# Beginning the attention of a second model's mixer earlier, with compression, gates and the first up products between its units

## The reference

```python
# xn: 256 x 1024, normed; projections of it by w_in: NSA queries (8 heads), keys and values of NSA,
# MoBA queries, keys, values (8 heads), 24 gate columns, two wide gates (2 x 1024 columns)
kc, vc = silu(blocks(k) @ ck_w1) @ ck_w2, silu(blocks(v) @ cv_w1) @ cv_w2     # compression
o_c = softmax(q @ kc.T) @ vc                                                  # compressed branch
y_nsa  = g0 * o_c + g1 * attend(q, k_sel, v_sel) + g2 * attend(q, k_win, v_win)   # g = sigmoid(24 columns)
y_moba = attend(q_m, k_m, v_m)
merged = sigmoid(gate_a) * (y_nsa @ w_up_nsa) + sigmoid(gate_b) * (y_moba @ w_up_moba)
x = x + merged @ w_out
```

## Time and profile before

| | |
|---|---|
| median of 3 runs (lowest, highest) | 1749.6 us (1748.1, 1751.0) |
| profiled execution | 1749.17 us, of which the span in the profile is 1747.4 us |
| PE busy | 1684.5 us, 96% |
| DVE busy | 1141.9 us, 65% |
| ACT busy | 892.0 us, 51% |
| mean granted PE clock | 0.991 |
| second mixer | kc's first product at 1273.05 us of the span, next norm's first product at 1518.31 us |

### The profile page before, as it was taken

How to read it: one execution, slowest core, us unless ns; L and a number is a source line. 1 busy time by engine, 2 the same in 40 slices (tenths; PEclk the granted TensorE clock), 3 DMA queues, 4 the chain that set the end, 5 groups by cost and what they waited for, 6 DMA issues and landing times.

```text
span 1747.4 us, 30010 instructions
## 1 busy us (share of the span) xinstructions
PE 1684.5 (96%) x12938; PEld 1544.5 (88%) x12938; DVE 1141.9 (65%) x1622; ACT 892.0 (51%) x1172; POOL 330.2 (19%) x387
## 2 busy tenths in 40 slices
PE   8999999999999997999999999999989899999998
PEld 7978999888999986899998878999978788899998
DVE  5556689756776679566666556767675657754555
ACT  6545555545456664455555545555544446444344
POOL 1211799501560016100000113010006000000000
PEclk9999999999999999999999999999999999999999
DMA  7436547465544653445555334655535521465551
GB/s 249 145 110 178 178 164 243 168 204 169 168 146 169 210 183 109 154 151 187 193 180 174 129 121 111 229 190 173 193 127 165 170 86 62 146 214 184 181 190 49
DMA packets 203396, 286.21 MB, mean 164 GB/s; under 512 B 6432, under 2 KB 162272, under 8 KB 203264
## 3 DMA queue, kind: packets, MB, share of 16 engines
q1 hardware_dynamic: 197584, 272.25, 47.1%
q0 software_dynamic: 2224, 5.75, 1.4%
q10 hardware_dynamic: 3456, 6.29, 1.1%
HBM read 279.03 MB, written 5.24 MB: 163 GB/s over the span
## 4 chain that ended last, share of the span: by engine, by line
PE 85%; DVE 9%; ACT 3%; issue 2%; POOL 1%; DMA 0%; ACTq 0%; SPq 0%; POOLq 0%; DVEq 0%
PE ps L106 84%; DVE wlo L118 3%; ACT arena L112 2%; DVE arena L118 1%; ACT whi L112 1%; PE ps L109 1%; DVE arena L136 1%; DVE xres L118 1%; POOL arena L118 1%; DVE arena L130 1%; POOL sm L118 1%; DVE arena L124 1%; DVE arena L121 0%; DVE sm L121 0%; DVE arena L127 0%
## 5 line engine op out<-in xcount | busy, mean ns | idle before, releaser
L118 DVE TENSOR_TENSOR wlo<-raw,whi 128x2048 fp32r<-128x2048 f32 (+2 forms) x259 | 603.1, 2336 | 294.9 <-ACT whi L112 294.7
L106 PE MATMUL ps<-xh,whi 128*128 128x256 f32 x2288 | 652.8, 285 | 5.3 <-DVE wlo L118 2.4
L106 PE MATMUL ps<-xl,whi 128*128 128x256 f32 x2288 | 648.6, 283 | 0.0
L106 PE MATMUL ps<-xh,wlo 128*128 128x256 f32 x2288 | 648.6, 283 | 0.0
L112 ACT ACTIVATE whi<-raw 128x2048 fp32r<-128x2048 f32 (+2 forms) x259 | 491.6, 1901 | 243.8 <-PE ps L106 241.0
L106 PEld LDWEIGHTS ps<-xh,whi 128*128 128x128 f32 x2288 | 440.0, 192 | 14.7 <-issue 8.9
L106 PEld LDWEIGHTS ps<-xl,whi 128*128 128x128 f32 x2288 | 440.2, 192 | 1.6
L106 PEld LDWEIGHTS ps<-xh,wlo 128*128 128x128 f32 x2288 | 440.1, 192 | 0.0
L106 PE MATMUL ps<-whi,oh 128*128 128x512 f32 (+1 forms) x640 | 249.0, 389 | 2.5 <-DVE wlo L118 1.8
L106 PE MATMUL ps<-wlo,oh 128*128 128x512 f32 (+1 forms) x640 | 247.0, 386 | 0.0
L106 PE MATMUL ps<-whi,ol 128*128 128x512 f32 (+1 forms) x640 | 246.4, 385 | 0.0
(11 more groups left out here) (150 smaller groups left out, 1704.9 us busy)
## 6 DMA issues: line engine op xcount, KB each, us to landing
raw<-in_ffn_w_up SPq DMA_DIRECT2D x88, 1024.0 KB, 5.1
raw<-in_ffn_w_down SPq DMA_DIRECT2D x44, 1024.0 KB, 5.0
raw<-in_sb_w_qkv SPq DMA_DIRECT2D x23, 1024.0 KB, 5.7
raw<-in_w_ffn_in SPq DMA_DIRECT2D x22, 1024.0 KB, 5.1
raw<-in_w_in SPq DMA_DIRECT2D x19, 1024.0 KB, 5.3
raw<-in_w_ffn_out SPq DMA_DIRECT2D x11, 1024.0 KB, 4.9
raw<-in_sb_w_o SPq DMA_DIRECT2D x8, 1024.0 KB, 5.0
raw<-in_sg_w_in SPq DMA_DIRECT2D x8, 1024.0 KB, 5.3
```

Of the source, the lines that this page charges most:

```text
L106: return NOP if self.e is None else self.e.matmul(*a, **k)
L118: return NOP if self.e is None else self.e.tensor_tensor(*a, **k)
```

## The change

**The first tile after a norm by k.** In `qk`, the state-space layer, the up products of every feed-forward net and `kc`, the first tile's 48 matmuls are no longer ordered m outside, k inside, but k outside and m inside (`feat_major_pair`), with the wait for piece k of the normed input (`xl`) ahead of each k. In `tok_major` (of these, the gating layer alone uses it with a wait) the wait for the last piece becomes one for each k:

```diff
     def tok_major(self, pe, w, nk, k0, nK, ah, al, outs, n, xl_of=None):
 
-        if xl_of is not None:
-            pe.wait_ge(*self.on("xl", xl_of, k0 + nk - 1))
         for k in range(nk):
+            if xl_of is not None:
+                pe.wait_ge(*self.on("xl", xl_of, max(k0 + k, 1)))
```

**The attention loop begins after turns 3 to 6**, and everything else goes into it:

```diff
-        block("mix", 24)
...
-        for p in range(3):
-            to_QT(p, ("rope_nsa",))
+        self.heads_turn_pe(pe, V, 5, ("qt_dve", 3))
+        self.heads_turn_pe(pe, V, 6, ("qt_act", 4))
         self.attend_pe(pe, N, V)
...
+    TURN = {4: 0, 5: 1, 6: 2}
+    C_TURN, C_HIDDEN, C_MEAN, C_ROPE, C_TABLES, C_SCORES, C_PROB, C_PC, C_VALUES, Y_SIDE = 7, 8, 9, 10, 11, 12, 13, 14, (18, 19), {15: 2, 16: 3}
...
+            if n < 24 and n % 2 == 0:
+                fronts(n)
+            if n < 4:
+                compress(*self.CMP[n])
+            elif n < 20:
+                gate(*divmod(n - 4, 2))
+            if n == 20:
+                w0 = self.tile(pe, "mup", 0)
+                pe.wait_ge(*self.on("gz_out", 7))
+                self.merge_pe(pe, w0, 0, 0)
+            if n == 21:
+                pe.wait_ge(*self.on("cmp_out", 1))
+                self.merge_pe(pe, w0, 0, 1)
+            if n == 24:
+                w2 = self.tile(pe, "mup", 2)
+                pe.wait_ge(*self.on("a_max", 22))
+                self.merge_pe(pe, w2, 2, 0)
```

```diff
+            if n < 4:
+                self.cut_hi(ac, ("cmp",) + self.CMP[n])
+            elif n < 20:
...
+            if n == 4:
+                ac.wait_ge(*self.on("tile", "cmp", 1, 1))
+                ac.activation(V["HT"], self.B[6][0:30, :], ACT_F.Silu).then_inc(*self.up("ht"))
...
+            if n < 4:
+                self.cut_lo(dv, ("cmp",) + self.CMP[n])
+            elif n < 20 and n % 2 == 0:
+                self.cut_lo(dv, ("gz", (n - 4) // 2))
...
+            if n == 2:
+                dv.wait_ge(*self.on("turn_rstd", 0))
+                self.scale_heads(dv, V, 0, 12).then_inc(*self.up("nsa_scaled"))
+            if n == 3:
+                dv.wait_ge(*self.on("nsa_scaled"))
+                self.rope_heads(dv, N, V, 0, 12, "rope_dve", ("rope_nsa",), "RSN")
```

More of the change, by code:

```diff
@@ L2041, in second_pe @@
-        pe.wait_ge(*self.on("vv_n", 1))
-        for p in range(3):
-            to_QT(p, ("rope_nsa",))
+        self.heads_turn_pe(pe, V, 3, ("rope_moba",))
+        self.heads_turn_pe(pe, V, 4, ("rope_moba",))
+        w = self.tile(pe, "mix")
+        pe.wait_ge(*self.on("head_out", "qn", 1))
+        for k in range(KT):
+            ins = self.mm3(pe, B[2][0:24, 0:256], w[0][:, k, :], w[1][:, k, :], self.xh[:, k, :], self.xl[:, k, :], k == 0, k == KT - 1)
+        ins.then_inc(*self.up("tile", "mix"))
@@ L2061, in second_pe @@
-        for i in range(1, 4):
-            self.out_proj_pe(pe, "second", i)
-    def y_turn_pe(self, pe, V, p, bank):
-        src = V["OA"].rearrange("p t h d -> p t (h d)")
-        if p == 0:
-            pe.wait_ge(*self.on("a_norm", 23))
-            pe.wait_ge(*self.on("gz_out", 7))
-        if p == 1:
-            pe.wait_ge(*self.on("ol", "y", 3))
-        if p == 2:
-            pe.wait_ge(*self.on("a_norm", 3))
-            pe.wait_ge(*self.on("cmp_out", 1))
-        if p == 3:
-            pe.wait_ge(*self.on("a_norm", 7))
-            pe.wait_ge(*self.on("ol", "y", 2))
+                self.merge_pe(pe, w, i, s)
@@ L2077, in y_turn_pe, with heads_turn_pe @@
+        for i in range(4):
+            self.out_proj_pe(pe, "second", i, [("gate_mul", 1, 1)])
+    def heads_turn_pe(self, pe, V, p, done):
+        pe.wait_ge(*self.on(*done))
         for k in range(2):
             for t in range(2):
-                kt = 2 * p + k
-                ins = pe.transpose(self.B[bank][:, k * 256 + t * P:k * 256 + (t + 1) * P], src[:, t, kt * P:(kt + 1) * P], self.ident[:, :])
+                j = 2 * p + k
+                ins = pe.transpose(self.B[self.QT_OUT[p][1]][:, k * 256 + t * P:k * 256 + (t + 1) * P],
+                                   V["QK"][:, t, 2 * j:2 * j + 2, :].rearrange("p a b -> p (a b)"), self.ident[:, :])
+        ins.then_inc(*self.up("qt_turned", p))
@@ new lines, in gate, with mix_turn @@
+        def gate(i, m):
+            if m == 0:
+                self.w_gate = self.tile(pe, "gz", i)
+                pe.wait_ge(*(self.on("gz_out", i - 1) if i else self.on("ht")))
+            ins = self.feat_major(pe, self.w_gate, m, 8, B[6][:, m * 256:(m + 1) * 256], self.xh, self.xl)
+            if m == 1:
+                ins.then_inc(*self.up("tile", "gz", i))
+        def mix_turn():
+            pe.wait_ge(*self.on("mix_sig"))
+            for t in range(2):
+                ins = pe.transpose(B[3][:, 24 * t:24 * t + 24], V["GTF"][:, t * P:(t + 1) * P], self.ident[0:24, 0:24])
+            ins.then_inc(*self.up("mix_turned"))
@@ L2283, in second_act @@
-        for i in range(1, 4):
+        ac.activation(V["GTF"], B[2][0:24, 0:256], ACT_F.Sigmoid).then_inc(*self.up("mix_sig"))
+        self.heads_turn_act(ac, V, 6)
+        self.attend_act(ac, N, V)
+        for i in (1, 3):
+            self.cut_hi(ac, ("mup", i))
+            for s in range(2):
+                s2 = i - 1 + s
+                ac.wait_ge(*self.on("gate_sum", s2))
+                ac.activation(self.xh[:, 2 * s2:2 * s2 + 2, :], V["GZ"][0][s2], ACT_F.Copy).then_inc(*self.up("oh", "second", s2))
@@ L2464, in second_dve @@
-        for i in range(1, 4):
+                s2 = i - 1 + s
+                gz = V["GZ"][0][s2]
+                self.gate_dve(dv, V, i, s)
+                dv.wait_ge(*self.on("gate_mul", i, s))
+                dv.tensor_tensor(gz, gz, V["GZ"][1][s2], ALU.add).then_inc(*self.up("gate_sum", s2))
+                dv.wait_ge(*self.on("oh", "second", s2))
+                dv.tensor_tensor(self.xl[:, 2 * s2:2 * s2 + 2, :], gz, self.xh[:, 2 * s2:2 * s2 + 2, :].bitcast(F32),
+                                 ALU.subtract).then_inc(*self.up("ol", "second", s2))
```

395 lines of the change are left out of this document (204 added, 191 removed).

## The result

The changed kernel takes 1775.9 us (median of 4 runs, 1772.5 to 1777.6) where the kernel before takes 1750.3 us (1748.1 to 1751.0): ratio 1.0145, 95% interval 1.0132 to 1.0158, 25.6 us slower. The forecast was slower by 13.7 us, 1763, with a range up to 1771.

The account below looks back on a forecast made before the run. The prediction took PE to bound the kernel before. Entry +13.5, gated units +3.2, tail -2.2 and first tiles by k -0.8 gave +13.7 us on 1749.17, so 1763 us; own range 1756 to 1769, with rivals 1750 to 1771.

Parts of the forecast that it names:

- The entry: End of `kvn` to first gate: DVE's serial iterations with cuts delay the first gate from 1366.79 to 1380.3, +13.5 us.
- The clock: Half clock behind the stall at the entry: 1.7 to 3.4 us more, 1.7 taken.
- The gated units: First gate to last: eight pairs at 9.5 us plus compressed-branch steps and turns, 85.4, with clock 87, against 83.9: +3.2 us.
- The 6.8 us of the paired fronts are lost here: Gated units: PE work saved by issuing two units' scores together is lost to the chain through DVE and ACT.
- The tail: Behind the gated units to the next norm: 65.4 us, 10.4 of it waits, against 67.6: -2.2 us.
- First tiles by k: Gating layer's 0.79 us wait for pieces of `xl` goes: -0.8 us, nothing taken elsewhere.
- Gate columns: 48 products at 0.11 us become 24 at 0.12, 2.9 us: -2.5 us of PE; first half-clock stretch goes, -3.4.
- the rule on turns: Tail, iterations 24 to 27: turns not counting as busy for the clock would add some 2 us; left out.
- PE bound behind the first gate: Rival, chance 0.10: a pair's chain is hidden, gated units cost 80 us, tail waits halve; +1.5, 1751 us.
- Faster: Rival, chance 0.06: first four units hidden, entry under 15 us, all PE savings count; -21 us, 1728.
- Worse: Rival, chance 0.14: half clock follows each longer wait and a pair's chain is 10.5 us; +7 to +12 more, 1770 to 1775.

Follow-up runs that it names:

- second: Changed kernel with ACT's weight cut moved ahead of the exponentials of its unit, n = 0 to 24: 1749.7 us, ratio 0.9997.
- ninth: Changed kernel with ACT's cut ahead of the exponentials in iterations 0 to 4 only: 1760.7 us, ratio 1.0068.
- third experiment: Changed kernel with 44 and 88 useless products filling PE's two long waits at the entry: 1771.4 us, ratio 1.0126.
- sixth: Changed kernel with ACT's cuts first, plus DVE's last cut and gate products and ACT's four sigmoids deferred behind the loop: 1743.3 us, ratio 0.9962.
- fifth experiment: Kernel before with only the first tiles ordered by k and the gating layer's wait for each k: 1749.8 us, ratio 0.9999.
- seventh: Changed kernel with ACT's cuts first, plus compression's silu taken in iteration 3 instead of 4: 1742.9 us, ratio 0.9967.
- fourth: Kernel before with only the scores of two units issued together at even n: 1748.0 us, ratio 0.9990.
- eleventh: Kernel before with paired scores and ACT's cut ahead of the exponentials: 1741.1 us, ratio 0.9952.
- first experiment: Changed kernel with the scores of each unit issued alone again: 1778.1 us, ratio 1.0160.
- eighth kernel: Changed kernel with ACT's cuts first, deferred tail, earlier silu, and second compressed-branch values an iteration later: 1732.9 us, ratio 0.9905.

## Why the prediction was wrong, and where it was right

**The entry** (+13.5): right in mechanism and size, +13.2. The maximum of unit 4 begins 36.0 us behind the end of `kvn` (forecast 36.4), DVE's cuts follow each other at 6.0, 5.9, 8.2 and 7.7 us where I had 6.1, 5.9, 8.25 and 7.85 for the iterations, the waits of 5.5 and 11.0 us for the maximum and the silu are the 5.7 and 12 that I had named, and the second and ninth experiments show that the series through ACT's cut makes them.

**The clock**: this step failed. I wrote "I take 1.7, as behind the shorter stretch", for one restart behind the first gate, and gave the clock behind the other waits to a rival at 0.14 (1770 to 1775). In the changed kernel six half tiles of products run wholly or partly at half clock: the one at 1381.61 takes 5.1 us, the others, at 1424, 1433, 1462, 1483 and 1504, take 4.4, 4.5, 4.3, 5.3 and 5.3, each where 2.95 is the normal length. That is 11.2 us over (28.9 less 6 x 2.95), 9.5 more than I had put in, of the 12.9 us between forecast and measurement. (Between the two profiled executions the gap is 14.4 us: beside the clock 2.5 lie ahead of the end of `kvn`, and 2.6 in the gated units and the tail, less 0.3 at the entry.) The waits that I had listed myself, 4 us at n = 21 and twice 2 us at the loop's end, are where the two windows of 6.8 us begin; I had priced the waits and not what follows them, though the earlier trace rows showed a wait of 2.9 us followed by 6.8 us at half clock. For the entry the third experiment shows the cause. For the tail the sixth takes the waits away and the window goes with them, which fits, but there the waits went by less work in the loop too. The windows of 3.4 us at 1424 and 1462 come behind short waits (0.6 and 0.8 us; 1.5 and 0.8 us), and what brings them was not tried; the third experiment at the first place and the ninth at both have the same waits and full clock. The one at 1434 follows the scores of the compressed branch, as the one at 1399.1 did before; the forecast, which took 1.7 us once for the mixer, had left that one out as well. The Trainium skill (TensorE: Matmul & The Clock Gate, HAM oscillation — how this bites in real kernels) describes this: a wait for data puts PE back to the slow clock and the work behind it starts cold. The trace agrees for the long waits, with 0.21 against 0.12 us between products behind the 10.96 us wait; the window at 1434 follows no wait.

**The gated units** (+3.2, measured +9.9): without the clock's 6.6 us in the four gate halves, it is 87.2 us against the 85.4 that I had before the clock: the stretch was sized within 2 us. Some of that is luck. PE's waits in it are 6.5 us, where 9.5 against 8.6 us in eight pairs makes 7.2: four for the gates' copies (2.8 us, ahead of four of the seven gate tiles behind the first and not nearly each), two for maxima (1.8), and two for DVE's steps of the compressed branch (1.9), of which I had listed none; the longer of these two, 1.4 us at n = 19, is the second in the list's third row. PE's own work was then 80.7 us, not 78.2. "The 6.8 us of the paired fronts are lost here" was right: the pairs are worth 2.2 us in the changed kernel, 2.1 in the kernel before (there in part because of more half clock), 12.6 where the chain is short.

**The tail** (-2.2, measured +3.3): 70.9 us, of which 4.7 are the clock; without it 66.2, against a forecast of 65.4. Waits as forecast: 4.0 us for `cmp_out`, 2.2 and 1.6 for the last units.

**First tiles by k** (-0.8): not found; the fifth experiment measures 0. In the changed kernel's profiled execution the part from the first product after the first norm to the end of `kvn` took 1326.8 us, 2.6 longer than before (1324.2), with two windows of 3.4 us at half clock in the gating layer and the one behind it (at 393 and 550 us) which the profile of before lacks. The fourteen traces together tell more. All eleven kernels with the order by k have one of these two windows, the changed kernel and the seventh both; the three without that order (before, the fourth, the eleventh) have neither. So half clock at these places goes with the new order, and I had no term for it. With one window the part takes 1323.7 to 1325.2 us (nine profiles), with none 1324.2 to 1324.9 (three), so one costs nothing that can be seen; with both it takes 1326.6 and 1326.8. Why two executions have both was not found; others with the same code there have one.

**Gate columns**: 2.84 us for the 24 products, forecast 2.9, without half clock, as forecast; hidden behind DVE, which sets the entry.

**The turns and the clock**: leaving the rule on turns out was right for this time. The sixth experiment has the same turns as the changed kernel in its tail, and its 60 us run at clock 1.00.

**The rivals.** "PE bound behind the first gate" was wrong as the first experiment shows. "Faster" named its condition, an entry of under 15 us; the eighth kernel turned out faster with one of 24.6 us. "Worse" had the right mechanism at too small a chance: it should have been part of the forecast, since every wait in it came from my own list. Its other half, a pair's chain of 10.5 us, did not come, so its 1770 to 1775 lies near the measured time partly by luck.

## What to carry to other kernels

When work of several engines is interleaved by hand, follow one iteration across the engines and look for what stands in series only because of its place in a list: here a cut that needs no result of the unit stood behind the unit's exponentials on ACT, and moving it ahead of them was worth 26 us, the half clock that went with PE's waits included. Less work on PE is worth little until the chain around it is shorter than PE's own work: the same edit gave 2 us and 13 us. And a wait of PE can cost more than its length. Behind each of the long waits of the second mixer (3.2 to 16.1 us, in six of the fourteen traces) products ran at half clock, so the half-clock stretch belongs into the sum for every such wait. Behind shorter ones it belongs into the range: the wait of 2.5 us ahead of the first scores is followed by half clock in three of nine kernels that have it, the one of 2.2 us ahead of the first gate in two of three.

## What the hardware showed that I had not expected

A wait of PE has a price behind it that can be saved by useless work: 132 products that nobody reads, laid into two waits of 5.5 and 11.0 us, took 3.7 us out of the gated stretch (median 1775.9 to 1771.4). And two products on different halves of the rows, in different banks, run side by side here as they did in the earlier trace rows: the scores of two units take 0.91 us, from 1371.36 to the gate at 1372.27 in the eighth experiment, where one unit alone took 0.85.

```profile
1371.36 0.93 PE L107 MATMUL ps<-arena 64*128 64x128 f32 x8
1372.27 0.36 PE L107 MATMUL ps<-xh,whi 128*128 128x256 f32 x1
```

The third thing needs no wait at all. The scores of the compressed branch are 32 records of products with 16 columns behind 6 of value products, 4.7 us in which the profile calls PE busy; during or behind them the clock halves in all fourteen traces (from 1399.1 before, 1408.7 in the eighth experiment), and the gate half that follows takes 4.0 to 5.3 us instead of 2.95. On PE's timeline of the eighth experiment, group of small products and then the gate's first:

```profile
1404.12 4.68 PE L107 MATMUL ps<-arena 128*128 128x64 f32 x38
1408.72 0.58 PE L107 MATMUL ps<-xh,whi 128*128 128x256 f32 x1
1409.11 0.42 PE L107 MATMUL ps<-xl,whi 128*128 128x256 f32 x1
```

Here it costs 1.5 us in the gate half behind it (4.5 us). Whether the small width brings it was not tried.
